# Five half-groups of a feed-forward layer as seven half-size block products each

## The reference, cut to what matters

```python
h = rms_norm(x, g_pre_mlp) * (1.0 + scale2) + shift2
f = einsum('ntd,df->ntf', h, w_ff1)        # 1024 -> 4096
f = einsum('ntf,fd->ntd', square(relu(f)), w_ff2)   # 4096 -> 1024
x = x + gate2 * rms_norm(f, g_post_mlp)
```

## Time and profile before

| | us |
|---|---|
| three runs | 1849.82, 1848.41, 1852.27 |
| median | 1849.82 |
| profiled execution, first to last instruction (its span) | 1852.6 |
| TensorE busy / VectorE / ScalarE / GpSimd | 1732.3 / 719.1 / 599.7 / 411.7 |

### The profile page before, as it was taken

The page is one execution under the profiler, slowest core; times in us unless marked ns, Lnnn a source line. Parts: engine busy times, 40 slices in busy tenths (PEclk is TensorE's granted clock), DMA queues, the critical chain, the costliest instruction groups (busy, mean ns, idle before and its releaser), DMA issues. The chain is left out here.

```text
span 1852.6 us, 25908 instructions
## 1 busy us (share of the span) xinstructions
PE 1732.3 (94%) x10828; PEld 1611.6 (87%) x10828; DVE 719.1 (39%) x1406; ACT 599.7 (32%) x1107; POOL 411.7 (22%) x254
## 2 busy tenths in 40 slices
PE   5799995899999999989999989999999999999997
PEld 2699994888778878768999989999989998999996
DVE  2412114646677878763364572111211121112235
ACT  3312213245455556542252452101211121012312
POOL 1545542100000000000244542221222122212521
PEclk9999997799999999998999999999999999999998
DMA  9344525311110100033622302111111111111422
GB/s 297 87 108 103 133 83 137 102 51 47 47 43 27 39 27 27 28 113 113 186 71 87 101 27 69 46 46 46 46 47 46 46 46 36 47 52 50 126 69 58
DMA packets 205704, 137.14 MB, mean 74 GB/s; under 512 B 44565, under 2 KB 201409, under 8 KB 205545
## 3 DMA queue, kind: packets, MB, share of 16 engines
q1 hardware_dynamic: 197867, 125.16, 23.6%
q10 hardware_dynamic: 7718, 10.29, 1.7%
HBM read 115.82 MB, written 21.92 MB: 74 GB/s over the span
## 5 line engine op out<-in xcount | busy, mean ns | idle before, releaser
L2162 POOL TENSOR_TENSOR ff_lo<-ff_raw,ff_hi 128x1024 fp32r<-128x1024 f32 x56 | 136.9, 2447 | 492.2 <-ACT ff_hi L1977 492.2
L1257 PE MATMUL gate_ps<-h_hi,gate_w_cut 128*128 128x344 f32 x768 | 227.1, 344 | 7.4 <-ACT gate_sum L1380 5.2
L1257 PEld LDWEIGHTS gate_ps<-h_hi,gate_w_cut 128*128 128x128 f32 x768 | 141.4, 193 | 14.5 <-ACT gate_sum L1380 7.7
L2341 PE MATMUL ff_acc<-h_hi,ff_hi 128*128 128x344 f32 x672 | 142.6, 321 | 0.6 <-DVE relu_c L2490 0.6
L2341 PE MATMUL ff_acc<-h_lo,ff_hi 128*128 128x344 f32 x672 | 142.6, 320 | 0.0
L2341 PE MATMUL ff_acc<-h_hi,ff_lo 128*128 128x344 f32 x672 | 141.9, 319 | 0.0
L1353 ACT ACTIVATE prob<-scores,bias 128x640 f32<-128x640 f32 (+7 forms) x192 | 106.0, 558 | 98.9 <-DVE bias L1421 52.1
L1977 ACT ACTIVATE ff_hi<-ff_raw 128x1024 fp32r<-128x1024 f32 x56 | 58.4, 1050 | 230.0 <-DMA ff_raw<-in_w_ff_dram 230.0
L2341 PE MATMUL ff_acc<-f_lo,ff_hi 128*128 128x344 f32 x576 | 124.0, 323 | 6.3 <-issue 6.3
L1448 DVE TENSOR_TENSOR p_lo<-pT,p_hi 128x512 fp32r<-128x512 f32 (+1 forms) x148 | 101.4, 686 | 66.9 <-ACT p_hi L1364 66.5
L2341 PE MATMUL ff_acc<-f_hi,ff_hi 128*128 128x344 f32 x576 | 123.8, 324 | 2.6 <-issue 2.6
(11 more groups left out here) (385 smaller groups left out, 3928.1 us busy)
## 6 DMA issues: line engine op xcount, KB each, us to landing
ff_raw<-in_w_ff_dram SPq DMA_DIRECT2D x56, 512.0 KB, 4.0
wa_rest<-in_w_ada_dram SPq DMA_DIRECT2D x16, 1024.0 KB, 5.3
gate_spill<-gate_sum SPq DMA_DIRECT2D x48, 172.0 KB, 1.9
gates<-gate_spill SPq DMA_DIRECT2D x16, 516.0 KB, 5.1
wa<-in_w_ada_dram SPq DMA_DIRECT2D x8, 1024.0 KB, 9.9
gate_w_raw<-in_w_in_dram SPq DMA_DIRECT2D x16, 512.0 KB, 4.1
w_raw<-in_w_in_dram SPq DMA_DIRECT2D x30, 256.0 KB, 6.4
xt<-in_x_prompt_dram ACTq DMA_DIRECT2D x4, 1024.0 KB, 9.4
```

Source lines behind the costliest of these rows:

```text
L1257: last = pe.matmul(gps[:, 0:CH], gw_cut[:, 1 - u % 2, a, k], h[:, k, c * CH:(c + 1) * CH], start=(k == 0 and n == 0), stop=(k == KD - 1 an ...
L2162: pool.tensor_tensor(lo, raw, hi.bitcast(F32), ALU.subtract).then_inc(wflo_ready, 1)
L2341: last = pe.matmul(accs[s][:, c, 0:CH], w[:, z % SLOTS, k], x[:, k, c * CH:(c + 1) * CH], start=(k == 0 and n == 0), stop=(k == KD - 1 and ...
```

## The change

Groups 1, 2 (up and down) and the up half of group 3 are done in another way: five phases `ph` 0 to 4, of which 0, 2 and 4 are up. A phase cuts its weight matrix into four quadrants of 512x512, its activations into four of 512 features x 516 tokens, and makes four output quadrants out of seven products of sums of quadrants. In the order of the code: P1 = W11 X11; P7, P6 and P5 with weight sums made in place in the quadrant "11" or "21" and activation sums kept in `tt`; P2 = W12 X21; P3 and P4. P7, P6 and P5 have no `start` flag: they add onto P1 in the same PSUM banks, so that the banks hold P1, P1+P7, P1+P7+P6, P1+P7+P6+P5 one after the other, each of which is taken by some engine. P2, P3 and P4 start afresh. What has to be added or subtracted at the taking is done by VectorE while it takes.

A product has four pieces of 128 output features; a piece is 4 x 3 x 2 = 24 matmuls of 258 columns into one of four pairs of PSUM banks. For a piece ScalarE cuts the high part of the weights (128x512), GpSimd makes the rest for pieces 0 and 2 and for all of P1 and P2, VectorE for the others. For each product ScalarE cuts the activations in two halves (128x1032), and VectorE makes their sums and rests, one product ahead.

The loop of three rounds is gone: the first down half-group is straight code with the old tiles, then come the 140 pieces as straight code, then `end` as before, with operands in other places. The weight quadrants are 1 MB each and are loaded as soon as the last rest made from the slot's former quadrant is done. Old slabs are reused: `quads` lies where h2_lo was, `h2r` (h2 put together again, `make_whole`) where h2_hi was, the rings of activation parts `xr` where f_hi was, the weight ring `wr` where ff_raw was.

```diff
+        ORDER = ("P1", "P7", "P6", "P5", "P2", "P3", "P4")
+        W_SUMS, X_SUMS = ("P7", "P6", "P5", "P3"), ("P7", "P6", "P5", "P4")
+        W_PART = {"P1": "11", "P7": "11", "P6": "11", "P5": "21", "P2": "12", "P3": "12", "P4": "22"}
...
+        def dve_takes(n):
+            return name not in ("P1", "P6") if is_upward(ph) else not (ph == 1 and name == "P1")
+        def act_takes(n):
+            return name in ("P1", "P6", "P5") if is_upward(ph) else ph == 1 and name == "P1"
+        def squared_piece(n):
+            return is_upward(ph) and name in ("P5", "P2", "P3", "P4")
+        def pool_rest(n):
+            return p % 2 == 0 or name in ("P1", "P2")
...
 (SyncE)
+                    def load_quad(ph, which):
+                        if ph == 0:
+                            sp.wait_ge(whole, 2 * s + 2)
+                        else:
+                            last = HK * product_at(ph - 1, {"11": "P5", "21": "P3", "22": "P3", "12": "P4"}[which]) + HK - 1
+                            sp.wait_ge(wrest_pool, n_pool_rest[last])
+                            sp.wait_ge(wrest_dve, n_dve_rest[last])
+                        sp.dma_start(quads[:, s], source_quad(ph, which)).then_inc(quad_loaded[s], 16)
...
 (ScalarE)
+                    for n in range(HK):
+                        w_piece_hi(n)                      # n < 4: waits for ff_done PLAIN - 3 + n
+                    for k in range(HK):
+                        x_part_hi(0, k, k + 1)             # waits for ff_done PLAIN
+                    for n in range(NPC):
+                        jj, p = divmod(n, HK)
+                        if HK <= n + 3 < NPC:
+                            w_piece_hi(n + 3)              # waits for st_done n, and for the weight sum
+                        if n and act_takes(n - 1):
+                            act_take(n - 1)
+                        elif n and squared_piece(n - 1):
+                            relu_piece(n - 1)              # waits for VectorE's take of n - 1
+                        if n >= 2 and squared_piece(n - 2):
+                            square_piece(n - 2)
+                        if p < 2 and jj + 1 < NPR:
+                            x_part_hi(jj + 1, 2 * p, 2 * p + 2)   # waits for the activation sum
...
 (GpSimd)
+                    for n in range(NPC):
+                        if pool_rest(n):
+                            pool.wait_ge(wphi_ready, n + 1)
+                            pool.tensor_tensor(wr[:, n % HK, 1], quad_piece(ph, W_PART[name], p), wr[:, n % HK, 0].bitcast(F32),
+                                               ALU.subtract).then_inc(wrest_pool, 1)
...
 (TensorE)
-                    with pe.Fori(0, NFG - 1) as q:
-                        for z in range(2 * KD):
...
+                    for n in range(NPC):
+                        jj, p = divmod(n, HK)
+                        ph, name, _ = piece(n)
+                        if pool_rest(n):
+                            pe.wait_ge(wrest_pool, n_pool_rest[n])
+                        else:
+                            pe.wait_ge(wrest_dve, n_dve_rest[n])
+                        if n < HK:
+                            pe.wait_ge(ff_taken[min(p, 1)], PLAIN // 2)
+                        else:
+                            if dve_takes(n - HK):
+                                pe.wait_ge(taken_dve, n_dve_taken[n - HK])
+                            if act_takes(n - HK):
+                                pe.wait_ge(taken_act, n_act_taken[n - HK])
+                        fresh = name in ("P1", "P2", "P3", "P4")
+                        for k in range(HK):
+                            if p == 0 and (jj == 0 or k % 2 == 0):
+                                pe.wait_ge(xlo_ready, x_steps(jj, k))
+                            for m, (a, b) in enumerate(((0, 0), (0, 1), (1, 0))):
+                                for c in range(2):
+                                    last = pe.matmul(banks[:, 2 * p + c, 0:HC], wr[:, n % HK, a, k], xr[:, jj % 2, b, k, c * HC:(c + 1) * HC],
+                                                     start=(fresh and k == 0 and m == 0), stop=(k == HK - 1 and m == 2),
+                                                     skip_group_check=True)
+                        last.then_inc(st_done, 1)
...
 (VectorE)
+                    x_part_rest(0, 0, 1)
+                    x_part_rest(0, 1, 2)
+                    gather(PLAIN - 1)
+                    x_part_rest(0, 2, 3)
+                    x_part_rest(0, 3, 4)
+                    for n in range(NPC):
+                        jj, p = divmod(n, HK)
+                        if n and dve_takes(n - 1):
+                            dve_take(n - 1)                # PSUM and SBUF, 128x516
+                        if HK <= n + 2 < NPC and not pool_rest(n + 2):
+                            w_piece_rest(n + 2)            # SBUF and SBUF, 128x512
+                        if n + HK < NPC and piece(n + HK)[1] in W_SUMS:
+                            w_sum(n + HK)                  # SBUF and SBUF, 128x512, in place
+                        if jj + 1 < NPR:
+                            if p == 0 and ORDER[(jj + 1) % len(ORDER)] in X_SUMS:
+                                x_sum(jj + 1, 0)           # SBUF and SBUF, 128x1032
+                                x_sum(jj + 1, 1)
+                            if p in (1, 2):
+                                x_part_rest(jj + 1, 2 * p - 2, 2 * p)   # SBUF and SBUF, 128x1032
+                        if jj == 4:
+                            mix(p + 1, y_tile(0, 1, p), y_tile(1, 1, p), y_tile(0, 1, p), ALU.subtract)   # 128x516; more in phase 4: P5, P2, P3
...
+                    dve_take(NPC - 1)
+                    for e in range(3, len(END_CUTS)):
+                        end_cut_rest(e)
```

More of the change, by code:

```diff
@@ L1760, in hybrid_step @@
         UPS = NFG * KD
-        NMAIN = 2 * UPS - NEARLY - KD
+        PLAIN = 2 * KD - NEARLY
         def part(x, c):
@@ new lines, in hybrid_step, with x_steps, x_sums, quadrant @@
+        n_wsum = upto(lambda n: piece(n)[1] in W_SUMS)
+        n_pool_rest, n_dve_rest = upto(pool_rest), upto(lambda n: not pool_rest(n))
+        def x_steps(jj, k):
+            return k + 1 if jj == 0 else HK + 2 * (jj - 1) + k // 2 + 1
+        def x_sums(jj, half):
+            return 2 * sum(ORDER[x % len(ORDER)] in X_SUMS for x in range(jj)) + half + 1
+        def quadrant(x, a, b, k0=0, k1=None):
+            k1 = HK if k1 is None else k1
+            return x[:, a * HK + k0:a * HK + k1, b * HT:(b + 1) * HT]
@@ L1853, in hybrid_step @@
         with ExitStack() as st:
-            accs = [psum(st, f"ff_acc{s}", [P, NCH, 512]) for s in range(2)]
-            tp = [psum(st, f"x_tp{i}", [P, 512]) for i in range(2)]
+            banks = psum(st, "ff_acc", [P, 8, 512])
+            accs = [banks[:, NCH * s:NCH * (s + 1)] for s in range(2)]
+            tp = [banks[:, 6 + i] for i in range(2)]
             bank = [accs[0][:, 0], accs[0][:, 1], accs[0][:, 2], accs[1][:, 0]]
@@ L1907, in _ @@
                     spill(2)
-                    for i in range(NEARLY, 2 * UPS):
+                    for i in range(NEARLY, 2 * KD):
                         load(i)
+                    for ph in range(NPH):
+                        for which in ("11", "21", "22", "12"):
+                            load_quad(ph, which)
+                    for t in range(NLATE):
+                        load_end(t)
+                    for t in range(NLATE, KD):
+                        load_end(t)
                     sp.wait_ge(spilled, 48)
@@ L2076, in end_square @@
+                    square_piece(NPC - 2)
+                    end_cut_hi(3)
+                    end_cut_hi(4)
+                    relu_piece(NPC - 1)
+                    square_piece(NPC - 1)
+                    end_cut_hi(5)
+                    end_w_hi(2)
+                    end_w_hi(3)
+                    for e in range(6, len(END_CUTS)):
+                        end_cut_hi(e)
+                    for t in range(NLATE, KD):
+                        end_w_hi(t)
                     def end_square(n):
@@ L2367, in end @@
                         if n == 0:
[L2368 to L2371, removed]
+                            before = lambda k: pe.wait_ge(elo_ready, k // 2 + 1 if k < HK else k - HK + 3)
+                        elif n == KD:
+                            pe.wait_ge(elo_ready, len(END_CUTS))
+                        _, hi, lo = end_weights(t)
+                        product(bank[n % 4], hi, lo, e_hi, f_lo, c, before).then_inc(end_done, 1)
                     def sum_y(c):
@@ L2588, in _ @@
+                    for m in range(PLAIN - 1):
                         if is_up(m):
```

303 lines of the change are left out of this document (270 added, 33 removed).

## The result

The changed kernel takes 1799.12 us (median of four runs, 1798.77 to 1803.02); the kernel before, on the same chip, 1849.12 (1847.63 to 1852.27). The ratio is 0.9726, 95% interval 0.9706 to 0.9745: faster by 2.7%, some 50 us. The forecast was 1788.6. The profiled execution spans 1801.2 us against 1852.6.

What follows compares the result with a forecast made beforehand. TensorE's matmuls were taken to bound the stage, other engines hidden. Span 1852.6 - 57.9 - 14.2 + 6.1 + 3.3 + 1.5 = 1791.4 us, so 1788.6 us median; own range 1782 to 1800, 8-in-10 range 1778 to 1814.

Steps and rivals of the forecast that it cites:

- columns, with extra waits: Feed-forward products: 140 pieces of 2.834 us replace tiles of 454.7 us, -57.9 us; extra waits of pieces and parts add 1.0.
- loop edges: Jumps back of the hardware loop: straight code removes both, with their idle time and half-clock matmuls, -14.2 us.
- entry: Before the first piece: TensorE waits for cuts and remainders, then runs at a low clock, +6.1 us (1.2 to 7.4).
- VectorE and GpSimd: Beside the products: GpSimd operations hold VectorE up, so TensorE waits in some products, +3.3 us (0 to 29.5).
- exit: After the last piece: ScalarE arrives late, a wait of 1.1 us as now, plus 0.5 for five hand-overs (0 to 6).
- Rival (d): Feed-forward matmuls shrink less: 258 columns cost what 264 do, 1798 us; chance 0.05.
- (a): In the products VectorE sets the pace, its slack used up by latencies between ScalarE and VectorE: 1815 us; chance 0.17.
- (b): Better than forecast: entry at its lower end and no later wait, 1779 us; chance 0.08.
- (c): Slower than before: late operands at heads of products idle TensorE and drop its clock repeatedly, up to 1889 us; chance 0.06.
- The weight quadrants: DMA loads during the products: 1 MB each lands in some 5.3 us, with 20 us of cover, costing nothing.

## Why the prediction came out so

The direction and the bound were right: TensorE's matmuls set the stage before and after, and VectorE stays hidden. The forecast span, 1791.4, is 9.8 us under the profiled one, by these terms. The 3.3 us of waits that never came hide part of the 12 us by which the columns and the exit were dearer than forecast; that is luck.

| term | forecast, us | measured, us |
|---|---|---|
| columns, with extra waits | -57.9 + 1.0 | 140 x 2.890 - 454.7 = -50.1 |
| loop edges | -14.2 | no break left; -14.2 |
| entry | +6.1 | +6.5 |
| VectorE and GpSimd | +3.3 | 0 |
| exit | +0.5 | +5.7 |
| later start of the stage (1128.10, 1127.45 before) | none | +0.65 |
| sum (measured spans: -51.4) | -61.2 | -51.45 |

- **The columns: the term that was mis-sized.** "A piece is 2.90 x 258/264 = 2.834 us" scales one row by its columns. The piece takes 2.890, 56 ns more, 7.8 us over 140. My upper end, 2.90, holds it. Rival (d) names the number (1798) but not the mechanism: 264 columns twice in the same loop cost 2.948, so 258 isn't rounded up to 264. That no fixed part can be seen between two rows said nothing on widths and places that neither row has.
- The estimate from the Trainium skill (TensorE: Matmul & The Clock Gate, "Wait - 56ns, not 53.3ns?"), a gain of 50.4 us, stands near the measured 50.1, but its levels don't: 110.0 ns at 258 columns where the starts lie 120.4 apart, and the three cuts above that share the same 516 columns differ by up to 1.8 ns per matmul.
- **The loop edges: right.** The written-out loop alone shows it in one chain.
- **The entry: the parts were right, the size partly by luck.** By the starts of matmuls, the first two pieces end 7.87 and 12.24 us after the last plain tile instead of 2.89 and 5.78, 6.5 us late. The idle is 2.71 us where 2.6 was forecast, the third x part comes at 5.1 where 5.0 was, and the clock then stands at 0.50. But eight other versions with the same entry lose 4.5 us in their profiles, where the clock rose sooner and the second idle didn't come (last section). The price of the low clock was half of "some 5.2 us", a length that rows 5 don't give: they have 0.50 from 1036 us on and 0.53 from 1041 to 1042, and the same trace has 0.56 from 1035 to 1036, so it lasted more than 6 us. The reordered entry shows that the fourth weight cut and the gather made the long idle and, by their order, the wait for the third part.
- **VectorE and GpSimd: nothing where 3.3 us were forecast.** That sum lets each GpSimd operation hold VectorE up in full; counted so, the version with all remainders on GpSimd would be 20 to 40 us slower, and its ratio, 0.972, is that of the change. In the rows a weight remainder on VectorE is longer by 0.13 us (814 against 683) and one on GpSimd by 0.52 (1811 against 1292): both pay, and VectorE is left with 60 us of 380. That the pieces were slower than forecast isn't the reason: at 2.846 us, with 256 and 260 columns, TensorE doesn't wait either. What holds of that step is that a take isn't held up. The Trainium skill (SBUF — State Buffer, "SBUF: two separate sides") puts it as an exclusive lock on a port pair, held for a whole instruction by whichever starts first, between a VectorE operation with two SBUF inputs and a GpSimd one that reads SBUF. The trace agrees: 682 to 688 ns for the takes in all versions, 683 and 1109 for the sums without and with GpSimd beside them.
- **Rivals (a), (b) and (c).** (a) and (c) would show VectorE without idle time and a low clock in the phases. VectorE has idle time before its takes (36.7 us before those into fraw alone), and the clock is 1.00 for all of 1280 to 1660 us. (b) needed an entry of 1.2 us; it cost 4.5 to 6.5. The Trainium skill tells of a kernel whose clock swung while it cycled through banks, with TensorE idle for short times between groups (TensorE: Matmul & The Clock Gate, "A second HAM failure mode: psum-queue depth-cycling"). Here some 130 pieces over four pairs of banks leave no such idles, TensorE being busy for all of 1280 to 1660 us at a clock of 1.00, so the trace has the cycling without its idles and without the swing.
- **The exit: the step that failed.** "ScalarE arrives some 2 us late, so the remainder comes at 4.8: a wait of 1.1" follows one queue, ScalarE's. The code puts `end_cut_rest(0)` ahead of the take of the last piece but one in VectorE's, and that remainder waits for a cut which ScalarE does after relu and square of the piece before. From the end of the last piece to the end of the span it is 125.6 us, from the end of the last tile before 119.9; the stated upper end of the term, 6, holds the 5.7. Moving the takes ahead gave back 4.8 of them, 3.97 by the 25th matmul of the exit. Of the other 0.9 most is TensorE's idle, 0.81, 0.37 and 0.70 us with the takes moved against 1.11 before; the 0.70 stands behind four remainders that take 11.71 us beside GpSimd's subtractions. The low clock at this place isn't what cost the time: with the entry alone reordered TensorE idles as long there, the clock stays at 1.00, and it is 125.6 us again.
- The weight quadrants land as forecast from the earlier trace rows, and no engine waits for them:

```profile
w_quads<-in_w_ff_dram SPq DMA_DIRECT2D x20, 1024.0 KB, 5.3
```

## What to carry to other kernels

Where TensorE is full, a change of tile width is worth what a piece of exactly that width, place and order measures: 56 ns on 2.83 us took a seventh of the columns' gain here, and a cut of 256 and 260 columns in place of 258 twice gave most of it back. At the seams between two stages, follow every queue in the order in which it is written, for an operation that is early in need but late in its operands holds all behind it; two reorderings of a few lines were worth half a per cent. And 130 subtractions moved from VectorE to GpSimd took 2 us of 318.5 off VectorE, for both engines read their two operands from SBUF and lengthened each other's work.

## What was not expected of the hardware

- **Matmul times that repeat to the nanosecond and differ by place.** In the phases the distances of starts run from 113 to 130 ns. Sorted by their place in a cycle of eight pieces (two x buffers, four pieces), those of one place agree to 0.3 ns (standard deviation over the phases), and the places differ by 3.1 (standard deviation too). They are the same to 0.4 ns whether or not GpSimd works beside them.
- **The same idle, two prices.** TensorE's wait before the first piece is 2.71 us in the changed kernel and in the eight others with its entry. In the changed kernel's profile the first matmul behind it starts at 1267.44 us, the granted clock is still 0.97 from 1268 to 1269, then 0.50, and 0.81 from 1275 to 1277, that is, full again at 1275.8; the first two pieces end 6.5 us late. With the exit reordered, and nothing else at the entry, the first matmul starts at 1268.32, and the clock is at 0.50 from 1269 and back at 0.97 in the stretch 1272 to 1275. There, as in the versions with other cuts or other remainders, the first piece ends 7.4 us after the last plain tile and the second its plain time later, 4.5 us late. The second idle, of 0.53 us, is seen in the changed kernel's profile only: with its first two x parts done at full pace TensorE had to wait for the third, and at the lower pace it had not. Whether that second idle kept the clock low isn't shown. An idle of 1.54 us cost no clock at all, and at the exit an idle of 2.63 us didn't either in the version with the entry reordered, where 2.64 us in the changed kernel did.

Stretches of the changed kernel, then of the reordered exit, then TensorE and a stretch at the exit with the entry reordered:

```profile
1268.00:1269.00 1.00, 1.00 (x10) 0.91 (x8) 1.00 (x2) 0.00 (x0) 0.00 (x0) 0.97 0.00 0
...
1275.00:1277.00 2.00, 2.00 (x16) 2.00 (x15) 1.63 (x2) 0.11 (x1) 2.00 (x1) 0.81 0.03 8
```

```profile
1272.00:1275.00 3.00, 3.00 (x27) 3.00 (x25) 3.00 (x4) 2.03 (x4) 0.36 (x1) 0.97 0.00 0
```

```profile
1676.23 0.44 PE L2489 MATMUL ff_acc<-e_hi,end_hi 128*128 128x384 f32 x1 [2.63 <-DVE f_lo L2984]
```

```profile
1676.00:1684.00 8.00, 7.04 (x37) 6.29 (x38) 5.02 (x8) 7.53 (x10) 3.58 (x2) 1.00 1.13 329
```
